# Twelve units of a projection in seven products instead of eight, in the first block of a three-block kernel

## What is computed

```python
xn = rms_norm(h, norm_in_g)
q, k, v, g_ret, x_lru, g_lru = jnp.split(xn @ w_in, IN_SPLITS, axis=-1)
q = rotary(q); k = rotary(k) * RET_HEAD_DIM ** -0.5
scores = einsum('qd,kd->qk', q, k) * decay_mat          # per head, causal
o_ret = group_norm_heads(scores @ v)                    # (computed chunk by chunk)
y_ret = o_ret * silu(g_ret)
xc = causal_depthwise_conv(x_lru, conv_w, conv_b)       # 4 taps
r, i = sigmoid(xc @ gate_a + b_a), sigmoid(xc @ gate_x + b_x)   # 8 blocks of 128
a = exp(-8 r softplus(-lru_lambda)); b = sqrt(1 - a*a) * i * xc
h_t = a_t h_(t-1) + b_t;   y_lru = h * silu(g_lru)
h = h + concat(y_ret, y_lru) @ w_out
```

## Time and profile before

| | us |
|---|---|
| median of three runs | 2059.18 |
| lowest, highest | 2058.50, 2060.09 |
| time of the profiled execution | 2056.59 |
| its span | 2054.8 |
| TensorE busy | 2020.2 |
| VectorE busy | 1124.1 |
| GpSimd busy | 1015.3 |
| ScalarE busy | 375.3 |

### The profile page before, as it was taken

How to read it: one execution, slowest core, us unless ns; L and a number is a source line. 1 busy time by engine, 2 the same in 40 slices (tenths; PEclk the granted TensorE clock), 3 DMA queues, 4 the chain that set the end, 5 groups by cost and what they waited for, 6 DMA issues and landing times.

```text
span 2054.8 us, 39352 instructions
## 1 busy us (share of the span) xinstructions
PE 2020.2 (98%) x16934; PEld 1900.2 (92%) x16934; DVE 1124.1 (55%) x1958; ACT 375.3 (18%) x777; POOL 1015.3 (49%) x775
## 2 busy tenths in 40 slices
...
GB/s 331 172 126 154 144 164 115 129 165 175 168 165 124 171 175 167 190 103 106 40 5 103 107 160 167 175 172 157 171 165 166 204 162 148 150 116 166 172 176 62
DMA packets 43878, 307.63 MB, mean 150 GB/s; under 512 B 5288, under 2 KB 5544, under 8 KB 7744
## 3 DMA queue, kind: packets, MB, share of 16 engines
...
## 4 chain that ended last, share of the span: by engine, by line
PE 91%; DVE 6%; issue 1%; ACT 1%; DMA 0%; DVEq 0%; SPq 0%
PE ps L587 57%; PE ps L252 15%; PE ps L311 5%; PE ps L249 3%; PE ps L271 1%; PE ps L286 1%; DVE sb_work L425 1%; PE ps L1658 1%; DVE sb_xn L2562 1%; DVE sb_work L418 1%; PE ps L1683 1%; PE ps L393 0%; DVE sb_h L788 0%; PE ps L2145 0%; PE ps L2292 0%
## 5 line engine op out<-in xcount | busy, mean ns | idle before, releaser
L587 PE MATMUL ps<-sb_work,sb_ring 128*128 128x128 f32 x3968 | 476.2, 275 | 0.3 <-DVE sb_work L1977 0.3
L587 PEld LDWEIGHTS ps<-sb_work,sb_ring 128*128 128x128 f32 x3968 | 459.4, 192 | 1.0 <-issue 0.5
L555 POOL TENSOR_TENSOR sb_table<-sb_ring 128x512 f32<-128x512 f32 x126 | 161.4, 1281 | 369.0 <-PE ps L587 189.8
L587 PE MATMUL ps<-sb_work,sb_table 128*128 128x128 f32 x2256 | 285.4, 275 | 0.0
L587 PEld LDWEIGHTS ps<-sb_work,sb_table 128*128 128x128 f32 x2256 | 268.4, 192 | 0.0
L558 POOL TENSOR_TENSOR sb_ring<-sb_ring 128x512 f32<-128x512 f32 x189 | 260.7, 1379 | 0.0
L557 POOL TENSOR_TENSOR sb_table<-sb_table,sb_ring 128x512 f32<-128x512 f32 x126 | 176.3, 1399 | 9.9
L587 PE MATMUL ps<-sb_xn,sb_ring 128*128 128x128 f32 x1440 | 175.5, 275 | 0.0
L587 PEld LDWEIGHTS ps<-sb_xn,sb_ring 128*128 128x128 f32 x1440 | 168.6, 192 | 0.4
L560 POOL TENSOR_TENSOR sb_table<-sb_ring,sb_table 128x512 f32<-128x512 f32 x126 | 168.4, 1336 | 0.0
L252 PE MATMUL ps<-sb_work,sb_ring 128*128 128x256 f32 x736 | 162.8, 380 | 0.0
...
## 6 DMA issues: line engine op xcount, KB each, us to landing
...
sb_table<-decay ACTq DMA_DIRECT2D x1, 1536.0 KB, 21.0
bias_rows<-sb_relg POOLq DMA_DIRECT2D x1, 1536.0 KB, 34.7
...
```

What stands on the lines that cost most here:

```text
L555: v.tensor_tensor(s[:, 0], a[1][0], a[1][1], ALU.add).then_inc(S["fw_ready"], 1)
L587: ins = mm(fast_bank(c, g, b)[:, i * P:i * P + P], *(sides[::-1] if token_major else sides), start=first and i == 0 and j == 0, stop=last ...
```

## The change

Units 4 to 15 are multiplied in the seven-product form. They get four pieces of new work: GpSimd prepares twelve units (the first work of its queue but for two small loads), VectorE spreads the input once, ScalarE copies twelve first products and VectorE makes twelve sums. The sums of a query or key unit land in SBUF, so that the half turn and the rotation read SBUF where they read PSUM before. The prepared sums use the table into which the decays of the retention were loaded at the start (1536 KB, from ScalarE's queue), and a work tile; the decays are now loaded in two halves behind the tenth and eleventh of the twelve units. On VectorE four of the eight convolution blocks move behind the first sums, and the exponential's wait on ScalarE moves ahead of two copies. The eight units of queries and keys and the four of values leave PSUM banks 0 to 3 as pairs (`fast_base`).

```diff
-    stages = [("b1_xlru", 4, 0), ("b1_q", 4, 0), ("b1_k", 4, 0), ("b1_v", 4, 0), ("b1_gret", 4, 0),
+    stages = [("b1_xlru", 4, 0), ("b1_q", 0, 4), ("b1_k", 0, 4), ("b1_v", 0, 4), ("b1_gret", 4, 0),
...
-FAST_ORDER = ["b2_ffn", "l0_ffn1", "l0_x", "l0_ffn2", "l1_ffn1", "gm", "l1_x", "l1_ffn2"]
+FAST_ORDER = ["b1_q", "b2_ffn", "l0_ffn1", "l0_x", "l0_ffn2", "l1_ffn1", "gm", "l1_x", "l1_ffn2"]
...
+        if name == "b1_q":
+            start, units, outs = PLAN[name][0], 12, 12
...
+def early_tile(c, z):
+
+    if z % PREPS < 2:
+        flat = c.table[:, :, :].rearrange("p a b -> p (a b)")[:, 1536 * (z % PREPS):1536 * (z % PREPS) + 1536]
+    else:
+        flat = c.work[4][:, :, :].rearrange("p a b -> p (a b)")[:, 0:1536]
+    return flat.rearrange("p (s k n) -> p s k n", s=3, k=4)
...
+    if z < FAST_Z["b2_ffn"]:
+        return early_tile(c, z)
...
+def fast_base(g):
+
+    return 2 * (g % 2) + (0 if g < FAST_G["b2_ffn"] else 4)
...
-    return c.ps[:, 4 + 2 * (g % 2) + b, :]
+    return c.ps[:, fast_base(g) + b, :]
@@ b1_scalar
+    act.wait_ge(S["b1_pad"], 2)
+    nc.scalar.activation(c.small[:, 8:16], c.small[:, 0:8], ACT.Exp, scale=-1.0).then_inc(S["b1_exp"], 1)
...
-    act.wait_ge(S["b1_abs"], 1)
-    nc.scalar.activation(c.small[:, 8:16], c.small[:, 0:8], ACT.Exp, scale=-1.0).then_inc(S["b1_exp"], 1)
...
-        c.wait_done(act, n0 + u)
+        copy_first(c, act, u)
+        act.wait_ge(S["fast_read"], u + 1)
-        nc.scalar.activation(c.hid[0:64, u % 2, :], c.bank(q0 + u)[64:128, :], ACT.Copy, scale=-1.0)\
+        head = W[u // 4][:, 2 * (u % 4):2 * (u % 4) + 2, :].rearrange("p a b -> p (a b)")
+        nc.scalar.activation(c.hid[0:64, u % 2, :], head[64:128, :], ACT.Copy, scale=-1.0)\
-        nc.scalar.activation(c.hid[64:128, u % 2, :], c.bank(q0 + u)[0:64, :], ACT.Copy)\
+        nc.scalar.activation(c.hid[64:128, u % 2, :], head[0:64, :], ACT.Copy)\
-    n0, q0 = PLAN["b1_v"]
-        c.wait_done(act, n0 + u)
-        c.read(nc.scalar.activation(v[:, :, u * 256:u * 256 + 256],
-                                    c.bank(q0 + u).rearrange("p (m n) -> p m n", m=2), ACT.Copy), q0 + u)
+        copy_first(c, act, 8 + u)
+        if u > 1:
+            c.wait_done(act, PLAN["b1_v"][0] + u - 1)
+            act.dma_start(c.table[:, 4 * u - 8:4 * u - 4, :], c.decay[:, 4 * u - 8:4 * u - 4, :])\
+                .then_inc(S["decay_loaded"], 16)
+        act.wait_ge(S["fast_read"], 9 + u)
+        nc.scalar.activation(v[:, :, u * 256:u * 256 + 256].rearrange("p t (i n) -> p i t n", i=2),
+                             c.t1[:, u % 2, :].rearrange("p (i t n) -> p i t n", i=2, t=2), ACT.Copy)\
+            .then_inc(S["b1_v_kept"], 1)
@@ b1_tensor
-    for u in range(8):
-        p_unit(c, pe, n0 + u, q0 + u, c.xn)
+    xt = W[3][:, :, :].rearrange("p a b -> p (a b)").rearrange("p (s k t) -> p s k t", s=4, k=4)
+    for u in range(12):
+        pe.wait_ge(S["fw_ready"], 4 * u + 4)
+        if u < 2:
+            for q in (2 * u, 2 * u + 1):
+                c.wait_read(pe, PLAN["b1_xlru"][1] + q)
+        else:
+            pe.wait_ge(S["fast_read"], u - 1)
+        fast_products(c, pe, n0 + u, u, range(4), lambda k, j, t: c.xn[:, 2 * k + j, t * P:t * P + P],
+                      lambda k, m: xt[:, m, k, :], u, True, True,
+                      (lambda: pe.wait_ge(S["b1_spread"], 4)) if u == 0 else None, u >= 8)\
+            .then_inc(S[f"unit_done{(n0 + u) % UNITS}"], 1)
         if u >= 5:
             lru_gates(u - 5)
-    n0, q1 = PLAN["b1_v"]
-    for u in range(4):
-        p_unit(c, pe, n0 + u, q1 + u, c.xn, token_major=True)
-        lru_gates(u + 3)
     lru_gates(7)
@@ scores, gates and outputs
+    pe.wait_ge(S["fast_read"], 11)
     gate_unit(0)
     gate_unit(1)
+    pe.wait_ge(S["fast_read"], 12)
@@ b1_vector
+    dve.wait_ge(S["xn_ready"], 8)
+    spread_input(c, dve, c.xn, W[3], S["b1_spread"], 0)
...
+    def head(u):
+        return W[u // 4][:, 2 * (u % 4):2 * (u % 4) + 2, :].rearrange("p a b -> p (a b)")
+
+    def summed(u, out):
+        fast_sum(c, dve, u, out, lambda: c.wait_done(dve, PLAN["b1_q"][0] + u), ch)
+
     def rotate(u):
-        _, q0 = PLAN["b1_q"]
-        dst = W[u // 4][:, 2 * (u % 4):2 * (u % 4) + 2, :].rearrange("p a b -> p (a b)")
+        dve.wait_ge(S["fast_read"], u + 1)
         dve.wait_ge(S["b1_half_turn"], 2 * u + 2)
-        c.read(v.tensor_tensor(dst, c.bank(q0 + u), c.c("cos"), ALU.mult), q0 + u)
-        ch.step(v.tensor_tensor(c.t1[:, u % 2, :], c.hid[:, u % 2, :], c.c("sin"), ALU.mult))
-        c.wait_read(dve, q0 + u)
-        v.tensor_tensor(dst, dst, c.t1[:, u % 2, :], ALU.add).then_inc(S["b1_rotated"], 1)
+        v.tensor_tensor(c.t1[:, u % 2, :], c.hid[:, u % 2, :], c.c("sin"), ALU.mult)
+        ch.step(v.tensor_tensor(head(u), head(u), c.c("cos"), ALU.mult))
+        v.tensor_tensor(head(u), head(u), c.t1[:, u % 2, :], ALU.add).then_inc(S["b1_rotated"], 1)
...
-    for b in range(8):
+    for b in range(4):
         conv(b)
     dve.wait_ge(S["b2_bias_mm"], 1)
     v.tensor_tensor(c.relg[0:8, :], c.ps[0:8, 5, 0:384], c.c("future")[0:8, :], ALU.add)\
         .then_inc(S["b2_bias_read"], 1)
     for u in range(8):
+        summed(u, head(u))
+        if u < 4:
+            conv(4 + u)
+        elif u > 5:
+            decay(u - 6)
         rotate(u)
-        if u >= 5:
-            decay(u - 5)
-    for n in range(3, 8):
-        decay(n)
+    for u in range(4):
+        if u > 1:
+            dve.wait_ge(S["b1_v_kept"], u - 1)
+        summed(8 + u, c.t1[:, u % 2, :])
+        decay(u + 2)
+    decay(6)
+    decay(7)
 
     prob = c.hid[:, :, :].rearrange("p a b -> p (a b)").rearrange("p (a b) -> p a b", a=2)
     dec = c.table
-    dve.wait_ge(S["decay_loaded"], 32)
+    dve.wait_ge(S["decay_loaded"], 48)
@@ build, queues of ScalarE and GpSimd
-            act.dma_start(c.table[:, :, :], decay).then_inc(S["decay_loaded"], 16)
...
+            prepare_weights(c, pool, "b1_q")
```

More of the change, by code:

```diff
@@ L502, in fast_counts @@
     for name in FAST_ORDER:
-        if name == "gm":
+        if name == "b1_q":
+            start, units, outs = PLAN[name][0], 12, 12
+        elif name == "gm":
             start, units, outs = PLAN["gm_v"][0], 22, 18
@@ L700, in fast_sum @@
     v, S = c.nc.vector, c.S
-    two = c.ps[:, 4 + 2 * (g % 2):6 + 2 * (g % 2), :].rearrange("p b n -> p (b n)")
+    two = c.ps[:, fast_base(g):fast_base(g) + 2, :].rearrange("p b n -> p (b n)")
     dve.wait_ge(S["fast_p1"], g + 1)
@@ L911, in lru_gates @@
         if n == 0:
-            pe.wait_ge(S["decay_loaded"], 32)
+            pe.wait_ge(S["decay_loaded"], 16)
         pe.wait_ge(S["b1_conv"], n + 1)
@@ L947, in outputs @@
             pe.wait_ge(S["b1_gate_i"], 8)
-            c.wait_read(pe, q1 + 3)
-            c.wait_read(pe, q1 + 2)
+            pe.wait_ge(S["b1_v_kept"], 4)
         else:
@@ L1067, in decay @@
         dve.wait_ge(S["b1_gate_i"], n + 1)
-        v.scalar_tensor_tensor(out=W[5][:, n, :], in0=tmp[:, 1, :], scalar=1.0, in1=W[5][:, n, :],
-                               op0=ALU.add, op1=ALU.mult).then_inc(S["b1_ix"], 1)
+        ch.step(v.scalar_tensor_tensor(out=W[5][:, n, :], in0=tmp[:, 1, :], scalar=1.0, in1=W[5][:, n, :],
+                                       op0=ALU.add, op1=ALU.mult))
         dve.wait_ge(S["b1_gate_ready"], 4 * n + 4)
@@ L1117, in recurrence @@
             dve.wait_ge(S["b1_mult"], 1)
-            dve.wait_ge(S["b1_ix"], 8)
         for n in (2 * p, 2 * p + 1):
@@ L1522, in conv_scalar @@
         if i:
-            copy_first(c, act, 2 * i - 2)
+            copy_first(c, act, FAST_G["b2_ffn"] + 2 * i - 2)
         tap0(i, 0)
@@ L1526, in conv_scalar @@
             keep(i - 1)
-            copy_first(c, act, 2 * i - 1)
+            copy_first(c, act, FAST_G["b2_ffn"] + 2 * i - 1)
         act.wait_ge(S["b2_tap"], 8 * i + 4)
@@ L1533, in conv_scalar @@
     for b in range(4):
-        copy_first(c, act, 2 * (FFI - 1) + b)
+        copy_first(c, act, FAST_G["b2_ffn"] + 2 * (FFI - 1) + b)
 def conv_vector(c, dve, V, ch):
@@ L1577, in conv_vector @@
         if i:
-            fast_sum(c, dve, 2 * i - 2, c.t1[:, i % 2, :], lambda: c.wait_done(dve, n0 + 2 * i), ch)
+            fast_sum(c, dve, FAST_G["b2_ffn"] + 2 * i - 2, c.t1[:, i % 2, :], lambda: c.wait_done(dve, n0 + 2 * i), ch)
             taps(i - 1, 1)
```

13 lines of the change are left out of this document (6 added, 7 removed).

## The result

The changed kernel takes 2072.85 us (median of 4 runs, 2068.67 to 2073.55), the kernel before 2059.06 us (4 runs, 2058.50 to 2060.09). The ratio is 1.0061 with a 95% interval of 1.0048 to 1.0074: slower by 0.6%, clear of the scatter, and inside the forecast range. The profiled execution is the fastest of the four, 2068.67 us with a span of 2066.8.

The account below looks back on a forecast made before the run. TensorE bounds the kernel now; VectorE, held by GpSimd, would make it wait. -7.9 + 11.6 + 8.5 = +12.2 us takes the profiled execution from 2056.59 to 2068.8; the median lies 2.6 above, so 2071, range 2060 to 2079.

Parts of the forecast that it names:

- TensorE's gain: Twelve units on TensorE take 6.25 us each instead of 6.91, 7.9 us less in all.
- The price of a crossing: A VectorE instruction meeting a GpSimd one, both on SBUF, loses about 0.95 us if large, 1.1 if tiny.
- Steps 1 and 2: GpSimd starts at 27.7 us; VectorE's small chain, nine or ten instructions held at 1.3, ends at 45.6, net cost nothing.
- the walk: Step-by-step timing of GpSimd, VectorE and TensorE up to `scores(0)`, +12.2 us; as it stands 2066 to 2076, chance 0.55.
- Step 3: Held convolution blocks delay VectorE's first sum to 63.0, so TensorE stalls 11.6 us before the third unit.
- Step 4: VectorE's rounds from sum 0 to sum 8 take 62.9 us; TensorE waits 8.5 us in all before five units.
- a lower clock: After its stall TensorE runs at half speed; third and fourth units end 2 us later, costing 0 to 2, likely 0.
- Step 5: Sum 8 releases the eleventh unit at 126.2; `scores(0)` starts at 141.3 instead of 129.2.
- The decays' reload: Two halves issued at about 132 and 137, needed at 150.6; costed at nothing, 2 us if the second takes 21.0.
- TensorE as the bound: Rival: TensorE stays the bound and the gain survives in part, up to 7.9 us; up to 2051.3, chance 0.10.
- half of the loss: Rival: small chain held less, stall before the third unit 2 to 6 us; 2059 to 2066, chance 0.2.
- the worse case: Rival: ScalarE is drawn in by the held VectorE and the decays' reload comes late; 2076 to 2082, chance 0.15.

Follow-up runs that it names:

- before_plus_prep: The kernel before, with GpSimd's 48 preparation instructions for twelve units added, results unused, TensorE waiting for each preparation before its plain unit; 2075.73 us, ratio 1.0088.
- tiny_prep: The changed kernel with GpSimd's four instructions per unit cut from 128 x 512 to 128 x 1, TensorE taking those weights from the ring; 2054.19 us.
- bias_behind: The changed kernel with GpSimd's store of the bias rows (1536 KB) held until the decays have landed; 2067.55 us, ratio 1.0042 against the kernel before.
- chain_early: The changed kernel with VectorE's small chain of 25 instructions moved ahead of the normalization's root; 2065.35 us, ratio 1.0031 against the kernel before.

## Why the prediction was right, point by point

- **TensorE's gain, 7.9 us.** Right to 0.1 us in the stretch, once nothing else costs: 7.8, 5.2 and 2.6 for twelve, eight and four units.
- **The price of a crossing.** Right: 1.20 for a tiny instruction, 1.38 to 1.45 for the convolution's. before_plus_prep and tiny_prep show that it is GpSimd's instructions and their length that do it. By the Trainium skill, "SBUF — State Buffer", section "SBUF: two separate sides", a VectorE instruction with two inputs in SBUF waits for the whole of a GpSimd instruction that reads SBUF, and so does one in a 2-port fast mode. The trace agrees for the held TENSOR_TENSOR rows. TENSOR_SCALAR, with one tensor input, is held as long (1.20 at 30.77); whether it ran in such a mode no row shows. The RECIPROCAL at 28.20, with one input, took 0.20, but it stands in a gap between two of GpSimd's instructions (28.14 to 28.22), where others pass as well. In bias_behind it falls just inside one, and is not held:

```profile
34.14 0.20 DVE L1053 RECIPROCAL sb_small<-sb_small 128x8 f32<-128x8 f32 x1
...
34.03 1.26 POOL L568 TENSOR_TENSOR sb_table<-sb_ring 128x512 f32<-128x512 f32 x1
```

- **Steps 1 and 2.** GpSimd started 10.8 us before unit 4 (11.5 predicted). The small chain ended at 44.3; by the start of unit 4, which was 1.5 us earlier than before, that is 6.6 us behind it, where the walk had 6.4. Twelve of its instructions were held, 1.07 to 1.20 us each, where the walk had nine or ten at 1.3.
- **Step 3.** The third unit was wanted at 37.65 + 12.5 = 50.15 and started at 61.45: 11.3 us, of which the trace shows 11.04 as the wait; predicted 11.6. chain_early shows that the small chain makes most of it.
- **Step 4.** From the end of sum 0 at 61.3 to that of sum 8 at 124.0 VectorE took 62.7 us; the walk had 62.9. TensorE lost 8.4 us in these rounds (62.7 us from the third unit to the eleventh, less 8 x 6.25 and 5 pairs of gates at 0.86), predicted 8.5. But only 4.6 of them are waits, before three units and not five: 1.5 and 1.7 went into the third and the sixth unit at a lower clock. The prediction had said that such a loss would be taken from later stalls and cost nothing by itself. The trace bears it out: between 61 and 124 us VectorE never waits for TensorE, so the slower units did not make its rounds longer.
- **Step 5.** 15.2 us from the eleventh unit to `scores(0)`, predicted 15.1. The sum up to there was +12.2 and became +11.7.
- **Behind it: the mis-sized term.** The decays' reload was costed at nothing, with 2 us as the case of a second half that takes 21.0. It took 20.57, and from `scores(0)` to `outputs(0)` went 2.4 us: 1.3 of waiting for it, 0.7 of a gap that the profile gives to issue, the rest in smaller pieces. The issue times were right (132 and 137 by the walk, 130.3 and 135.5 with unit 4 1.5 us earlier). The reason that it was slow was not named: the store of the bias rows, which by the prediction moves to 121 and has no price there, ran from 119 to 155 beside it. bias_behind moved the store behind the decays, and they landed in 4.1 us. The ratios give this edit 3.9 us, the profiled executions 2.4; the profiled one of the changed kernel was its fastest by 4.2 us, and how late the load came in the others no trace shows. The gap of 0.7 is there also in chain_early (0.78) and not in tiny_prep, all three with the store beside; its cause stays open.
- **The time.** +11.7 and +2.4 make the +14.2 of the stretch; the walk had +12.2. The profiled execution took 2068.67, where 2068.8 was forecast, with unit 4 started 1.5 us earlier than in the profile of before; the other three runs lie 4.2 to 4.9 above it, where 2.6 had been assumed. Hence a median of 2072.85 instead of 2071. That the profiled execution met the forecast to 0.1 us is luck: the stretch was 2.0 us longer than in the walk, the start 1.5 shorter, and the rest some 0.6 shorter. That the time fell into the range is not, since the two losses came where the walk had them and about as large (11.3 and 8.4 us, predicted 11.6 and 8.5).
- **The rivals.** TensorE as the bound and half of the loss did not come. Of the worse case the late reload came, at a small size. ScalarE was drawn in, but only where it cost little: the last three sums waited 1.64 to 1.71 us for its copy of the first product (L676), which stood behind the gates' activations, and the second half was issued 5.1 us after the unit that it waited for. Nothing was held there any more, as GpSimd's last preparation had ended at 119.3, and no unit of TensorE waited for these sums.
